# A hybrid decoder step on one core: selection steps moved from ahead of the first down projection to behind it, and one buffer for each part of the first group's up tiles

## The chip, the core and the metric

The kernel runs on one core of a Trainium2 chip. The core has TensorE (PE in the rows; PEld is its loading of weights), VectorE (DVE), ScalarE (ACT), GpSimd (POOL) and the queue of SyncE (SP), which here issues most of the transfers. The metric is the device time of one execution in microseconds (us). A profiled execution leaves a trace; its times count from the start of the span, which is the time from the first to the last instruction.

## The reference, cut to what matters

One layer of a decoder for a prompt of 1040 rows (16 of them learned) and 64 sample rows (8 sequences of 8): a recurrent branch and a sparse attention branch are merged through gates, projected and added to x; a gated feed-forward network with a causal convolution of width 3 follows. For each sample row the attention reads only the 256 past keys with the highest score.

```
def trunk_layer(x, pos, attend, shift_prev, s_prev, conv_prev, lp):
    h = rms_norm(x, lp['norm1_g']) @ lp['w_in']
    p_r, p_a, g_r, g_a = split_cols(h)
    y_r, s_fin, shift_last = rwkv7_branch(p_r, shift_prev, s_prev, lp)
    q, k, v, qi, wi, ki = dsa_project(p_a, pos)
    y_a = attend(q, k, v, qi, wi, ki)
    merged = (jax.nn.sigmoid(g_r) * (y_r @ lp['w_br_rwkv'])
              + jax.nn.sigmoid(g_a) * (y_a @ lp['w_br_attn']))
    x = x + merged @ lp['w_out']
    f, conv_last = conv_ffn(rms_norm(x, lp['norm2_g']), conv_prev, lp)
    x = x + f
...
def conv_ffn(h, conv_prev, lp):
    u = h @ lp['w_up']
    a, b = u[..., :D_FF], u[..., D_FF:]
    ext = jnp.concatenate([conv_prev.astype(a.dtype), a], axis=1)
    c = lp['conv_b'] + ext[:, 0:T] * lp['conv_w'][0]
    for j in range(1, CONV_W):
        c = c + ext[:, j:j + T] * lp['conv_w'][j]
    y = (jax.nn.gelu(c, approximate=False) * b) @ lp['w_down']
    return y, ext[:, T:]
...
    _, idx = lax.top_k(score, n_top)
```

D_MODEL is 1024, D_FF is 2816, everything is float32.

## The kernel before

The change lies in `tail`, the last part of the program, which runs from about 1395 us to the end. It works through the 1104 rows in three groups g of 368 columns (x is held transposed, so rows of x are columns here). For each group there are four stages on TensorE: the **branch** (16 products, two for each of the 8 channel tiles, merged by VectorE under the gates), the **projection** (8 output tiles, `out`; VectorE adds each to x in `project`), the **up tiles** (22 of them, f; each has a half a for the convolution and a half b) and the **down tiles** (8, t; VectorE adds each to x in `add_down`). After the projection and after the down tiles a norm is taken: ScalarE squares each tile, TensorE sums the squares over the partitions (`sum_tile`, L2177), ScalarE takes the root, VectorE inverts it and scales (`scale`). For the second norm of a group the sum of squares of down tile t stands in TensorE's order right behind down tile t + 1. In the second group the squares of tiles 1 to 5 are added on VectorE instead (`total`, L2927).

Every engine works off its own list of instructions in the order in which the code is written, and meets the others only through semaphores: nothing is reordered at run time. TensorE writes into three banks in turn, and a bank is free again when its reader has said so.

The **up tiles of the first group** are built otherwise than those of the second: all but the first are made of seven products of half size (`up_block`, L2295 and on), from sums of weights (WF) and of x (XF) that were made before. ScalarE takes the parts out of the banks into f1, f6, f5, f7, f4, f3 (`keep_block`), GpSimd adds them up into f16 and f167 and from these into the right half of a (AF) and the two halves of b (BC) (`finish_up`), ScalarE makes the three taps of the convolution from AF (`taps`), GpSimd adds the taps and multiplies by the gate. Each of the eight parts has two buffers, used in turn by even and odd f; AF has two as well, and its first two columns, which are the end of the group before (zero in the first group), are set to zero once.

The **selection** runs on VectorE beside all this. The scores of a sample row lie in two halves on 128 partitions, 4100 to a partition, and the 256 highest of each are found 8 at a time: 32 rounds of three steps, a maximum (L2878, MAX8), an index search (L2881, FIND_INDEX8 with its MATCH_VALUE_LOAD) and a replacement of the found values (L2884, MATCH_REPLACE8, with two small copies). That makes 96 steps, numbered 0 to 95; `steps(a, b)` writes the steps a to b - 1 into VectorE's list at that place. Behind step 95 stand the lists (`lists`), which turn indices into addresses; GpSimd carries parts of them over in the second group's up tiles, behind its work on tile f = 5 (LISTED) and the next, and TensorE transposes the result before up tile 14 (FLIP). GpSimd then gathers the keys and values, which TensorE uses from up tile 16 on.

The places of the steps before: 0 to 3 in the first group's branch, 4 to 10 in its projection, 11 to 61 behind its first norm (beside the up tiles of TensorE), 62 to 65 behind down tile 0, 66 to 77 two at a time behind the down tiles 1 to 6, 78 to 81 in the second group's branch, 82 to 84 in its projection behind tiles 1, 3 and 5, 85 to 95 behind its first norm.

## Time and profile before

| | |
|---|---|
| median of 3 runs | 2758.75 us (2757.34 to 2759.09) |
| the profiled execution | 2757.01 us |
| its span | 2755.2 us, 49283 instructions |
| TensorE busy | 2587.2 us, 94% |
| VectorE busy | 1738.1 us, 63% |
| ScalarE busy | 786.1 us, 29% |
| GpSimd busy | 390.5 us, 14% |
| maximum L2878, 32 times | 141.8 us, 4432 ns each |
| index search L2881, 32 times | 141.5 us, 4423 ns each |
| replacement L2884, 32 times | 141.2 us, 4413 ns each |

The busy times are sums over the whole span. Which engine sets the end differs from stage to stage, so they are to be read together with the chain of waits and with the timelines of a stage: in a timeline each row is an instruction, or several alike one after the other, with its start, its duration, and in brackets the idle time ahead of it on its engine and what ended that.

### The profile page before, as it was taken

The page shows a single profiled execution, that of the slowest core. Times are in us where ns is not written, and L with a number is a line of the kernel's source. Part 1 is how long each engine was busy: PE and PEld are TensorE (multiplying, and loading weights), DVE is VectorE, ACT ScalarE, POOL GpSimd, SP SyncE. Part 2 cuts the span into 40 slices and gives each one's busy share as a digit, 9 for nine tenths or more (in the row PEclk, how much of TensorE's full clock was granted, in tenths as well). Part 3 has the DMA queues.
Part 4 walks back from the last instruction along what each step waited for, and adds up shares of the span by engine and source line. Part 5 has one row for each costly group of instructions (what it writes and reads, how often), then busy time and mean ns, then how long its engine had stood idle before and what let it go on. Part 6 is the DMA issues. An engine that isn't in the chain of part 4 may idle for free.

```text
span 2755.2 us, 49283 instructions
## 1 busy us (share of the span) xinstructions
PE 2587.2 (94%) x19336; PEld 1784.8 (65%) x19336; DVE 1738.1 (63%) x3313; ACT 786.1 (29%) x1704; POOL 390.5 (14%) x575
## 2 busy tenths in 40 slices
PE   8998999999997997898899996899999999999997
PEld 5553566666654323788757995455665665679997
DVE  3555888864533457666679999967762322357666
ACT  2224322125443663111112551012334421122212
POOL 0000111000000000000002662000336451011111
PEclk9999999999998986999999998899999999999999
DMA  8882112131113540000245663244337563533332
GB/s 294 309 291 83 41 70 81 69 98 37 49 49 125 176 143 17 19 11 12 95 134 181 245 241 108 73 148 152 110 108 241 193 198 107 187 130 123 123 122 73
DMA packets 95959, 348.78 MB, mean 127 GB/s; under 512 B 19560, under 2 KB 43976, under 8 KB 74032
## 3 DMA queue, kind: packets, MB, share of 16 engines
q1 hardware_dynamic: 83696, 294.50, 31.1%
q0 software_dynamic: 12032, 51.14, 5.7%
q8 instruction: 153, 2.51, 0.4%
q14 instruction: 78, 0.64, 0.1%
HBM read 289.57 MB, written 55.23 MB: 125 GB/s over the span
## 4 chain that ended last, share of the span: by engine, by line
PE 43%; DVE 10%; DVEq 4%; issue 1%; DMA 1%; ACT 0%; POOL 0%; ACTq 0%; POOLq 0%; SPq 0%
PE banks L2359 6%; PE banks L2274 5%; PE banks L2292 5%; PE tl_P L2359 4%; DVE arena L2884 3%; DVE tl_v L2878 3%; DVEq L2882 3%; PE rc_P L1395 3%; PE tl_P L2274 2%; PE banks L2206 2%; PE banks L2218 2%; PE tl_P L2292 2%; PE banks L1407 1%; PE tl_P L2206 1%; PE tl_P L2417 1%
## 5 line engine op out<-in xcount | busy, mean ns | idle before, releaser
L437 PE MATMUL dp_PS<-base,dp_W 128*128 128x368 f32 x1440 | 465.9, 476 | 0.0
L437 PEld LDWEIGHTS dp_PS<-base,dp_W 128*128 128x128 f32 x1440 | 265.8, 190 | 157.5 <-issue 8.8
L162 PE MATMUL pa_PG<-pa_W,base 128*128 128x402 f32 (+1 forms) x576 | 199.1, 506 | 7.9 <-DMA pa_W<-in_w_dsa 7.9
L736 DVE TENSOR_SCALAR_CACHE_REDUCE dp_EQ<-dp_SCORE,dp_trial 128x1024 f32<-128x1024 f32 (+1 forms) x186 | 175.9, 946 | 19.9 <-issue 0.9
L162 PEld LDWEIGHTS pa_PG<-pa_W,base 128*128 128x128 f32 (+1 forms) x576 | 107.2, 187 | 94.7 <-issue 14.3
L2274 PE MATMUL banks<-base,tl_WU 128*128 128x368 f32 x496 | 158.8, 477 | 0.8 <-DVE base L2937 0.8
L2292 PE MATMUL banks<-base,tl_WD 128*128 128x368 f32 x484 | 156.2, 479 | 0.0
L2878 DVE MAX8 tl_v<-arena 128x8 f32<-128x4100 f32 x32 | 141.8, 4432 | 3.3 <-issue 1.5
L2881 DVE FIND_INDEX8 tl_i<-tl_v,arena 128x8 uint32<-128x4100 f32 x32 | 141.5, 4423 | 0.0
L2884 DVE MATCH_REPLACE8 arena<-tl_v,arena 128x4100 f32<-128x4100 f32 x32 | 141.2, 4413 | 0.3 <-issue 0.3
L2828 POOL DMA_INDIRECT arena<-in_cache_kv,tl_PHT x128 | 122.3, 955 | 109.7 <-PE tl_P L2438 73.6
L2274 PEld LDWEIGHTS banks<-base,tl_WU 128*128 128x128 f32 x496 | 94.4, 192 | 60.0 <-issue 3.6
L2292 PEld LDWEIGHTS banks<-base,tl_WD 128*128 128x128 f32 x484 | 91.6, 192 | 58.3 <-issue 5.9
L2543 ACT ACTIVATE arena<-base 128x368 f32<-128x368 f32 x44 | 22.1, 509 | 295.7 <-DVEq L2921 143.2
L814 DVE CUSTOM_DVE_ANT_0 dp_P<-dp_PS,dp_SCORE 128x1024 f32<-128x1024 f32 (+7 forms) x64 | 48.5, 758 | 66.7 <-PE dp_PS L487 58.8
L2304 PE MATMUL banks<-arena 128*128 128x184 f32 x504 | 85.6, 319 | 1.4 <-DVE arena L3052 1.4
L2218 PE MATMUL banks<-base,arena 128*128 128x368 f32 x256 | 81.2, 473 | 1.1 <-issue 1.1
L2304 PEld LDWEIGHTS banks<-arena 128*128 128x128 f32 x504 | 80.0, 190 | 1.6 <-issue 1.6
L2206 PE MATMUL banks<-arena 128*128 128x368 f32 x240 | 77.3, 473 | 2.0 <-DMA arena<-in_wb 1.2
L2274 PE MATMUL tl_P<-base,tl_WU 128*128 128x368 f32 x240 | 76.8, 473 | 0.0
L2510 POOL TENSOR_TENSOR base<-tl_T 128x368 f32<-128x368 f32 x36 | 30.3, 842 | 326.7 <-ACTq L2593 325.7
L594 ACT ACTIVATE dp_PMT<-dp_PS,dp_rest 128x368 f32<-128x368 f32 x42 | 23.8, 568 | 164.8 <-PE dp_PS L437 164.8
(525 smaller groups left out, 5057.4 us busy)
## 6 DMA issues: line engine op xcount, KB each, us to landing
tl_WU<-in_wu SPq DMA_DIRECT2D x58, 1024.0 KB, 4.9
pa_WQ<-in_wu SPq DMA_DIRECT2D x22, 1024.0 KB, 8.3
wsum<-pa_WS SPq DMA_DIRECT2D x22, 1024.0 KB, 4.9
tl_WD<-in_wd SPq DMA_DIRECT2D x32, 704.0 KB, 4.3
arena<-wsum SPq DMA_DIRECT2D x21, 1024.0 KB, 7.0
dp_W<-in_w_rw SPq DMA_DIRECT2D x15, 1024.0 KB, 4.9
arena<-in_wb SPq DMA_DIRECT2D x24, 512.0 KB, 3.7
arena<-in_wo SPq DMA_DIRECT2D x24, 512.0 KB, 3.8
```

The costliest lines, as they stand in the source:

```text
L162: last = pe.matmul(PG[0:n, c, 0:NC4], xT[:, k, r:r + n], W[:, c, k, :], start=k == 0, stop=k == KD - 1)
L437: last = pe.matmul(bank(f)[:, 0:w], W[:, t // 2 % 2, k, 128 * (t % 2):128 * (t % 2) + 128], xT[:, k, c:c + w], start=k == 0, stop=k == KD - 1)
L736: dve.tensor_scalar(EQ[0:n, 0:m], scored_of(j), values(n, x), None, op, ALU.add, accum_out=result[0:n, x:x + 1])
L2206: last = pe.matmul(out[:, 0:W], WM[:, i % 2, o:o + 128], YT[:, j, k, :], start=k == 0, stop=k == 3)
L2218: last = pe.matmul(out[:, 0:W], WM[:, i % 2, 128 * k:128 * k + 128], MT[:, k, :], start=k == 0, stop=k == KD - 1)
L2274: last = pe.matmul(out[:, 0:W], WU[:, i % 2, o:o + 128], XN[:, k, :], start=k == 0, stop=k == KD - 1)
L2292: last = pe.matmul(out[:, 0:W], WD[:, i % 3, 128 * e:128 * e + 128], HT[:, f, :], start=f == 0, stop=f == NF - 1)
L2304: last = pe.matmul(out[:, 0:H], weights[:, k, :], moving(k), start=first and k == 0, stop=k == 3, skip_group_check=True)
L2359: last = pe.matmul(out[:, 0:H], weights[:, k, :], moving(k), start=first and k == 0, stop=k == kk - 1, skip_group_check=True)
L2878: dve.max(v8[:, :], SC)
L2881: dve.max_index(i8[:, :], v8[:, :], SC)
L2884: dve.match_replace(SC, v8[:, :], SC, TAKEN)
```

## The change

Three things change; the work itself stays the same.

- **Steps.** 11 to 51 stand behind the first group's first norm (41 steps instead of 51), 52 to 72 three at a time behind the down tiles 0 to 6 (21 instead of 16), 73 to 76 in the second group's branch (4 as before), 77 to 83 one at a time behind tiles 0 to 6 of its projection (7 instead of 3), 84 to 95 behind its first norm (12 instead of 11).
- **Buffers.** f1, f6, f5, f7, f4, f3, f16 and f167 have one buffer each. ScalarE waits before it writes f1 of a tile until GpSimd has made f167 of the tile before (the new semaphore `f_mid`), and before it writes f5 until GpSimd has finished BC of the tile before (`b_read`). Before, one wait at the head of `keep_block` asked for the tile before the last.
- **First columns of AF.** They are copied from AL on ScalarE for every tile, in `taps`; the setting to zero on GpSimd is gone. AL is zero in the first group.

The functions now take the group as an argument, and a table `UPS = (NF, 1)` says in which group the seven products are used. With these values that is the first group alone, as before, and every bank and every transfer stays as it was.

```
+UPS = (NF, 1)
...
-        "PF": arena[:, 11872:14816].rearrange("p (i a n) -> p i a n", i=8, a=2),
-        "AF": arena[:, 14816:15556].rearrange("p (a n) -> p a n", a=2),
+        "PF": arena[:, 14048:15520].rearrange("p (i n) -> p i n", i=8),
+        "AF": arena[:, 15520:16260].rearrange("p (a n) -> p a n", a=2),
...
-                def taps(f):
-                    s = f % 2
+                def taps(g, f):
+                    s, i = f % 2, NF * g + f
                     w0, w1, w2, cb = (cw[:, k, f:f + 1] for k in range(4))
-                    if f >= 2:
-                        act.wait_ge(convolved, f - 1)
-                    act.wait_ge(f_right, f)
+                    act.activation(AF[:, s, 0:2], AL[:, f, :], ACT.Copy)
+                    if i >= 2:
+                        act.wait_ge(convolved, i - 1)
+                    act.wait_ge(f_right, block_no(g, f))
                     act.drain()
...
-                def keep_block(f):
-                    s = f % 2
-                    if f >= 3:
-                        act.wait_ge(b_read, f - 1)
-                    keep(f1[:, s, :], FA, fa_made, fa_taken, 2 * f - 1)
+                def keep_block(g, f):
+                    s, m = f % 2, block_no(g, f)
+                    FA, FD, FB = banks_of(g)
+                    if m > 1:
+                        act.wait_ge(f_mid, m - 1)
+                    keep(f1, FA, fa_made, fa_taken, 2 * m - 1)
                     if f > 1:
-                        taps(f - 1)
-                    keep(f6[:, s, :], FB, fb_made, fb_taken, 2 * f - 1)
-                    keep(f5[:, s, :], FD, fd_made, fd_taken, 2 * f - 1)
...
+                        taps(g, f - 1)
+                    keep(f6, FB, fb_made, fb_taken, 2 * m - 1)
+                    act.wait_ge(b_read, NF * g + f)
+                    keep(f5, FD, fd_made, fd_taken, 2 * m - 1)
...
-                pool.memset(AF[:, :, 0:2], 0.0)
...
-                    pool.tensor_tensor(f167[:, s, :], f1[:, s, :], f7[:, s, :], ALU.add)
-                    pool.drain()
...
+                        pool.tensor_tensor(f167, f1, f7, ALU.add)
+                        pool.drain().then_inc(f_mid, 1)
...
                             if g == 1:
-                                steps(78 + u // 4, 79 + u // 4)
+                                steps(73 + u // 4, 74 + u // 4)
...
-                            if g == 1 and t % 2 == 1:
-                                steps(82 + t // 2, 83 + t // 2)
+                            if g == 1:
+                                steps(77 + t, 78 + t)
...
-                        steps(11, 62)
+                        steps(11, 52)
...
-                        steps(85, 96)
+                        if UPS[1] > 1:
+                            mix_rows(XF, xf_done, False)
+                        steps(84, 96)
...
-                            if t == 0:
-                                steps(62, 64)
                             if t < KD - 1:
-                                steps(64 + 2 * t, 66 + 2 * t)
+                                steps(52 + 3 * t, 55 + 3 * t)
```

The order of VectorE's instructions shows where the steps stand. Line numbers after the change are 23 higher here (L2878 is L2901, L2881 is L2904, L2884 is L2907, `add_down` L2920 is L2943, `project` L2914 is L2937, `total` L2927 is L2950). Around the additions of the first group's down tiles 0, 1 and 2 VectorE has, before:

```order
L2881 MAX_INDEX tl_i<-tl_v,arena 128x8
L2920 TENSOR_TENSOR base<-base,tl_P 128x368
L2884 MATCH_REPLACE arena<-tl_v,arena 128x4100
L2885 COPY arena<-tl_v 128x8
L2886 CAST arena<-tl_i 128x8
L2878 MAX tl_v<-arena 128x8
L2881 MAX_INDEX tl_i<-tl_v,arena 128x8
L2884 MATCH_REPLACE arena<-tl_v,arena 128x4100
L2885 COPY arena<-tl_v 128x8
L2886 CAST arena<-tl_i 128x8
L2920 TENSOR_TENSOR base<-base,banks 128x368
L2878 MAX tl_v<-arena 128x8
```

Tile 0 is added behind step 61 and four steps follow. VectorE has there, after:

```order
L2901 MAX tl_v<-arena 128x8
L2943 TENSOR_TENSOR base<-base,tl_P 128x368
L2904 MAX_INDEX tl_i<-tl_v,arena 128x8
L2907 MATCH_REPLACE arena<-tl_v,arena 128x4100
L2908 COPY arena<-tl_v 128x8
L2909 CAST arena<-tl_i 128x8
L2901 MAX tl_v<-arena 128x8
L2943 TENSOR_TENSOR base<-base,banks 128x368
```

Tile 0 is added behind step 51, ten steps sooner, and between two additions stands one whole round. In the second group's projection VectorE has from tile 1 to tile 4, before:

```order
L2914 TENSOR_TENSOR base<-arena,banks 128x368
L2881 MAX_INDEX tl_i<-tl_v,arena 128x8
L2914 TENSOR_TENSOR base<-arena,banks 128x368
L2927 TENSOR_TENSOR tl_TOTAL<-tl_TOTAL,arena 128x368
L2914 TENSOR_TENSOR base<-arena,tl_P 128x368
L2927 TENSOR_TENSOR tl_TOTAL<-tl_TOTAL,arena 128x368
L2884 MATCH_REPLACE arena<-tl_v,arena 128x4100
L2885 COPY arena<-tl_v 128x8
L2886 CAST arena<-tl_i 128x8
L2914 TENSOR_TENSOR base<-arena,banks 128x368
```

A step stands behind every second tile. VectorE has from tile 1 to tile 4, after:

```order
L2937 TENSOR_TENSOR base<-arena,banks 128x368
L2901 MAX tl_v<-arena 128x8
L2937 TENSOR_TENSOR base<-arena,banks 128x368
L2950 TENSOR_TENSOR tl_TOTAL<-tl_TOTAL,arena 128x368
L2904 MAX_INDEX tl_i<-tl_v,arena 128x8
L2937 TENSOR_TENSOR base<-arena,tl_P 128x368
L2950 TENSOR_TENSOR tl_TOTAL<-tl_TOTAL,arena 128x368
L2907 MATCH_REPLACE arena<-tl_v,arena 128x4100
L2908 COPY arena<-tl_v 128x8
L2909 CAST arena<-tl_i 128x8
L2937 TENSOR_TENSOR base<-arena,banks 128x368
```

A step stands behind every tile.

## Rows read from the trace of the kernel before

**Rows 1.** Chain of waits in order of time: start us, us, what.

```profile
1694.44 4.43 DVE tl_v L2878
...
1708.24 4.43 DVE tl_v L2878
...
1752.49 13.61 PE tl_P L2292 x44
```

**Rows 2.** Timeline of TensorE, first group's down tiles 1 to 4.

```profile
1687.57 13.77 PE L2292 MATMUL banks<-base,tl_WD 128*128 128x368 f32 x44
1732.34 1.59 PE L2177 MATMUL tl_P<-arena,tl_ones 128*128 128x368 f32 x2 [31.00 <-ACT arena L2543]
1733.72 15.61 PE L2292 MATMUL banks<-base,tl_WD 128*128 128x368 f32 x44
...
1752.33 13.77 PE L2292 MATMUL tl_P<-base,tl_WD 128*128 128x368 f32 x44
...
1766.55 13.77 PE L2292 MATMUL banks<-base,tl_WD 128*128 128x368 f32 x44
```

**Rows 3.** Timeline of VectorE, the same stage to its last addition.

```profile
1685.23 4.42 DVE L2881 FIND_INDEX8 tl_i<-tl_v,arena 128x8 uint32<-128x4100 f32 x1
...
1731.11 0.54 DVE L2920 TENSOR_TENSOR base<-base,tl_P 128x368 f32<-128x368 f32 x1
1731.86 0.09 DVE L2884 MATCH_VALUE_LOAD arena<-tl_v,arena 128x8 f32 x1 [0.21 <-issue]
...
1823.02 0.54 DVE L2920 TENSOR_TENSOR base<-base,banks 128x368 f32<-128x368 f32 x1 [4.25 <-PE banks L2292]
```

**Rows 4.** Timeline of VectorE, the second group's projection.

```profile
1871.84 0.54 DVE L2914 TENSOR_TENSOR base<-arena,tl_P 128x368 f32<-128x368 f32 x1
...
1887.08 0.09 DVE L2884 MATCH_VALUE_LOAD arena<-tl_v,arena 128x8 f32 x1
...
1891.87 0.54 DVE L2914 TENSOR_TENSOR base<-arena,banks 128x368 f32<-128x368 f32 x1
...
1895.56 0.54 DVE L2914 TENSOR_TENSOR base<-arena,banks 128x368 f32<-128x368 f32 x1 [2.40 <-PE banks L2218]
...
1896.97 4.43 DVE L2878 MAX8 tl_v<-arena 128x8 f32<-128x4100 f32 x1
1901.55 0.54 DVE L2914 TENSOR_TENSOR base<-arena,tl_P 128x368 f32<-128x368 f32 x1
...
1905.46 0.54 DVE L2914 TENSOR_TENSOR base<-arena,banks 128x368 f32<-128x368 f32 x1 [2.61 <-PE banks L2218]
```

**Rows 5.** Timeline of TensorE, the second group's up tile 16.

```profile
2074.51 1.15 PE L2417 MATMUL tl_P<-ident,arena 128*128 128x128 f32 x8 [2.53 <-DMA arena<-in_cache_kv,tl_PHT]
2075.45 6.76 PE L2274 MATMUL banks<-base,tl_WU 128*128 128x368 f32 x16
```

**Rows 6.** Busy time by stretch: PE, PEld, DVE, ACT, POOL, PEclk, DMA share, GB/s.

```profile
2076.00:2077.00 1.00, 1.00 (x3) 0.65 (x2) 0.00 (x0) 0.75 (x3) 0.69 (x2) 0.50 0.97 385
```

**Rows 7.** Timelines of VectorE and GpSimd, the first list's hand-over.

```profile
1967.38 0.29 DVE L2946 TENSOR_SCALAR arena<-arena 64x256 f32<-64x256 f32 x1
...
1971.81 0.96 POOL L2526 TENSOR_TENSOR base<-base 128x368 f32<-128x368 f32 x1 [0.24 <-issue]
1973.40 0.64 POOL L2815 DMA_DIRECT2D arena<-arena  x1 [0.62 <-issue]
```

**Rows 8.** Timelines of GpSimd and ScalarE, an up tile of the first group.

```profile
1559.09 0.58 POOL L2804 TENSOR_TENSOR arena<-arena 128x184 f32<-128x184 f32 x1 [0.18 <-issue]
...
1560.98 0.58 POOL L2791 TENSOR_TENSOR base<-arena 128x184 f32<-128x184 f32 x1
...
1560.82 0.33 ACT L2609 ACTIVATE arena<-tl_P 128x184 f32<-128x184 f32 x1 [0.98 <-PE tl_P L2304]
...
1562.82 0.19 ACT L2621 ACTIVATE tl_AL<-arena 128x2 f32<-128x2 f32 x1
1563.11 0.54 ACT L2609 ACTIVATE arena<-banks 128x184 f32<-128x184 f32 x2
```

More of the change, by code:

```diff
@@ L1954, in tail @@
         f1, f6, f5, f7, f4, f3, f16, f167 = (M["PF"][:, i] for i in range(8))
-        FA, FD, FB, FE = R2, R0, R1, K0
-        FREED_D, FREED_B, FREED_A = 0, 1, 2
+        by_seven = lambda g, f: 1 <= f < UPS[g]
+        plain = [(g, f) for g in range(2) for f in range(NF) if not by_seven(g, f)]
+        nth = lambda g, f: plain.index((g, f)) + 1
+        block_no = lambda g, f: f if g == 0 else UPS[0] - 1 + f
+        FE = K0
         LROW = WU[:, :, :].rearrange("p i n -> p (i n)")[:, 0:3 * D].rearrange("p (b n) -> p b n", b=3)
@@ L1993, in tail @@
             if g < 2:
-                order += [(x, g, f) for f in range(NF if g else 1) for x in "ab"] + [("down", g, t) for t in range(KD)]
+                order += [(x, g, f) for f in range(NF) if not by_seven(g, f) for x in "ab"] + [("down", g, t) for t in range(KD)]
         use = {k: n for n, k in enumerate(order)}
@@ L2003, in tail @@
         uses = [sum(1 for n in use.values() if n % 3 == r) for r in range(3)]
-        uses0 = [sum(1 for n in use.values() if n % 3 == r and n <= use["b", 0, 0]) for r in range(3)]
+        uses0 = lambda g, r: sum(1 for n in use.values() if n % 3 == r and n <= use["b", g, 0])
+        nth_bank = lambda g, n: (use["a", g, 0] + n) % 3
+        banks_of = lambda g: [RB[nth_bank(g, n)] for n in (2, 0, 1)]
         NBL = len(BLOCKS3)
@@ L2138, in _ @@
                         load_up(NF * g + 1)
-                    if g == 0:
-                        load_sums(1)
-                        load_sums(2)
+                    if g < 2 and UPS[g] > 2:
+                        load_sums(g, 1)
+                        load_sums(g, 2)
                     if g:
@@ L2718, in _ @@
                         continue
-                    if g == 0:
-                        read_a(0, 0)
-                        read_b(0, 0)
-                        for f in range(1, NF):
-                            keep_block(f)
-                        taps(NF - 1)
-                    for f in range(NF if g else 0):
+                    if UPS[g] > 1:
+                        read_a(g, 0)
+                        read_b(g, 0)
+                        for f in range(1, UPS[g]):
+                            keep_block(g, f)
+                        taps(g, UPS[g] - 1)
+                    for f in range(UPS[g] if UPS[g] > 1 else 0, NF):
                         if g == 1 and f >= F0:
@@ L2806, in _, with finish_up @@
-                finish_up(NF - 1)
-                conv_add(pool, 0, NF - 1)
-                gate_up(pool, 0, NF - 1)
-                for f in range(BY_POOL):
-                    conv_add(pool, 1, f)
-                    if f:
-                        gate_up(pool, 1, f - 1)
+                def finish_up(g, f):
+                    s, m = f % 2, block_no(g, f)
+                    pool.wait_ge(fd_taken, 2 * m)
+                    pool.tensor_tensor(AF[:, s, 2 + H:2 + W], f16, f3, ALU.add).then_inc(f_right, 1)
+                    pool.tensor_tensor(BC[:, s, half[1]], f167, f5, ALU.add)
+                    pool.wait_ge(fe_taken, m)
+                    pool.tensor_tensor(BC[:, s, half[0]], f167, f4, ALU.add)
+                    pool.drain().then_inc(b_read, 1)
@@ new lines, in up_tiles @@
+                def up_tiles(g):
+                    for f in range(1, UPS[g]):
+                        m = block_no(g, f)
+                        if f > 1:
+                            finish_up(g, f - 1)
+                        pool.wait_ge(fa_taken, 2 * m - 1)
+                        pool.wait_ge(fb_taken, 2 * m - 1)
+                        pool.tensor_tensor(f16, f1, f6, ALU.add)
+                        conv_add(pool, g, f - 1)
+                        gate_up(pool, g, f - 1)
+                        pool.wait_ge(fb_taken, 2 * m)
+                        pool.tensor_tensor(f167, f1, f7, ALU.add)
+                        pool.drain().then_inc(f_mid, 1)
+                        if g == 1:
+                            hand_on(f)
+                    finish_up(g, UPS[g] - 1)
+                    conv_add(pool, g, UPS[g] - 1)
+                    gate_up(pool, g, UPS[g] - 1)
@@ L2813, in _, with hand_on @@
+                def hand_on(f):
                     if f == LISTED:
@@ L2820, in _ @@
                         pool.dma_start(K2[64:128, :], key[:, 128:256]).then_inc(spread, 16)
-                gate_up(pool, 1, BY_POOL - 1)
+                up_tiles(0)
+                if UPS[1] > 1:
+                    up_tiles(1)
+                for f in range(BY_POOL if UPS[1] <= 1 else 0):
+                    conv_add(pool, 1, f)
+                    if f:
+                        gate_up(pool, 1, f - 1)
+                    hand_on(f)
+                if UPS[1] <= 1:
+                    gate_up(pool, 1, BY_POOL - 1)
                 pool.wait_ge(placed_list, 1)
```

127 lines of the change are left out of this document (58 added, 69 removed).

## The prediction

> **What bounds the kernel now.** I read the chain of waits first, in order of time [rows 1]. Up to the first group's down projection, and after it, the chain lies mostly on TensorE (PE in the rows). Through the first group's up tiles and beyond it lies on VectorE (DVE), on one maximum, index search and replacement of the selection after the other, of which rows 1 show two maxima; it comes back to TensorE's down tiles only at 1752.49. The second view is TensorE's own timeline of those tiles [rows 2]. Down tile 1 starts at 1687.57, so tile 0's product was complete then. Tile 1 ends near 1701.2, and the next instruction, tile 0's sum of squares (L2177), starts at 1732.34 after 31.00 us of idle time. The third view says why [rows 3]: the addition of tile 0 (L2920) runs at 1731.11 on VectorE, 43.5 us after its product was there, because `steps(11, 62)` stands ahead of it in VectorE's order. From there to the sum of squares of the last tile, VectorE's additions set the pace and then catch up: the addition of tile 7 starts at 1823.02, with TensorE again the slower one. So the stage to cost runs from 1685 to 1823, and the question is what the moved steps do in the places that they go to.
>
> **The down tiles of the first group: 33.0 us gained.** In the changed order the loop ahead of tile 0 ends after step 51, a maximum. The next step, an index search, began at 1685.23 [rows 3], so VectorE is free then, 2.3 us before tile 0 is complete; TensorE's up tiles ahead of it are not moved. The addition of tile 0 comes at about 1687.8 and the 31.00 us are gone. Behind each of the tiles 0 to 6 there are now three steps, one whole round. A round takes 1708.24 - 1694.44 = 13.80 us [rows 1], the addition with its hand-over 1731.86 - 1731.11 = 0.75 us [rows 3]; with 0.05 for the end of the last step I take 14.6 us a tile. TensorE needs 1766.55 - 1752.33 = 14.22 us a tile [rows 2], and 0.6 less for the first, which has no sum of squares. So VectorE now sets the pace, by 0.4 us a tile. The addition of tile 7 starts at 1687.8 + 7 x 14.6 = 1790.0 instead of 1823.02: 33.0 us. Were TensorE alone in it, that would be 1687.8 + 13.6 + 6 x 14.22 = 1786.7; the round of steps costs 3.3 us of what could be had. A round with a tenth more in it, from a stall in fetching instructions, makes 32.3; I keep 32.3 to 33.4.
>
> **The second group's branch: nothing.** Four steps before and four now, 78 to 81 against 73 to 76. The kinds differ by one maximum that becomes an index search, 4.43 us [rows 4] against 4.42 [rows 3].
>
> **The second group's projection: 7.7 us lost.** Here three steps become seven, one behind each of the tiles 0 to 6. On before's clock tile 0's addition (L2914) starts at 1871.84 [rows 4]. Prices from the same rows: a replacement up to the next addition 1891.87 - 1887.08 = 4.79, a maximum 1901.55 - 1896.97 = 4.58, an index search taken like the maximum at 4.6; an addition alone 0.75, and with the running total 1896.97 - 1895.56 = 1.41. The order from tile 0 on is replacement, maximum, index search, replacement, maximum, index search, replacement, with totals from tile 2 on: 5.54 + 5.33 + 6.01 + 6.20 + 5.99 + 6.01 + 6.20 = 41.3 us. The addition of tile 7 then starts at 1871.9 + 41.3 = 1913.2, against 1905.46 before. TensorE has its eight products ready at the old pace, so the whole 7.7 us lie on the path: the sum of squares, the root, the scaling and the first up tile of the second group all wait for that addition. Only the loads of x and of the output weights stand behind VectorE too, and they lead by a tile or more.
>
> **TensorE's clock: 4.2 us lost, the least certain term.** Both lags make TensorE wait with nothing to do, about 4 us before the second group's branch and about 8 us (in two pieces) before its up tiles. Such waits are seen in the trace: after 2.53 us of idle time before 2074.51 the next 16 matmuls took 6.76 us, where 44 take 13.77 (so 16 take 5.0), and the granted clock was 0.50, the 1.2 GHz level [rows 5, 6]. After the 31.00 us, 44 matmuls took 15.61 instead of 13.77 [rows 2]. So one such wait costs 1.7 to 1.8 us if nothing covers it. I take 1.2 for the first, as the branch's first products have a little room while VectorE scales, and 3.0 for the second, since the transposes of the row output and then the first up tile run at the lower level one after the other. Bounds: 0, if the clock stays; 8, if each wait costs twice 1.8 and VectorE's work behind it slips too. The sum goes by 4.2.
>
> **One step more behind the scaling: nothing.** Twelve steps instead of eleven stand ahead of the lists, so the first instruction of the lists moves from 1967.38 to about 1972.0 on the stage's own clock [rows 7]. What takes the list up is GpSimd (POOL), which works off a convolution and a gate until 1971.81 + 0.96 = 1972.8 and issues its transfer at 1973.40 [rows 7]. The cover is some 0.4 us; beyond it the lists would slip by what is over, and TensorE meets them only nine up tiles later.
>
> **One buffer each for the parts of the up tiles: nothing.** ScalarE (ACT) now waits twice a tile for GpSimd. The second sum of parts ends at 1559.09 + 0.58 = 1559.67, and ScalarE writes f1 again at 1560.82; the last half of BC is done at 1560.98 + 0.58 = 1561.56, and f5 is written after 1563.11 [rows 8]. So the new waits are met 1.1 and 1.5 us early. The added copy of two columns is like L2621, 0.19 us [rows 8]; it shifts ScalarE and then GpSimd by about that and leaves 0.9 and 1.3 us. What would be late next is TensorE's second product into the same bank. The price with no cover is 21 tiles times what is missing. The Trainium skill speaks against this edit: its front page, "Trainium Kernel Development and Optimization", section Best Practices, says to double-buffer for performance, overlapping transfers with compute. By that rule every tile would show a wait; by the rows the reader has finished before the writer comes, and the sum goes by the rows.
>
> **Sum.** 33.0 - 7.7 - 4.2 = 21.1 us. The profiled execution took 2757.01 us, of which the span is 2755.2 and the rest lies around it, unchanged; that makes 2735.9. The median of the runs, 2758.75, is 1.7 above it, which makes 2737.7, say 2738 us.
>
> **Rivals.** (A) *The clock stays up* or the slow matmuls are all hidden: 25.3 us gained, 2733.5. For it: TensorE has some room behind both waits. Against: 2.53 us of idle time was enough [rows 5]. (B) *VectorE is later than costed*: rounds of 14.0 instead of 13.8 and a projection in which the slower clock and the steps add up, 8 us in place of 4.2 for the clock and 2 us more of lag: about 15 us gained, 2744. (C) *Another wait stands behind the removed one*: the weights of the down tiles, three buffers deep, might not arrive at 14.2 us a tile, and TensorE would wait for them instead. The tiles from 1752.33 on run at that pace without such a wait [rows 2], so this is unlikely; it would leave within 0.2% of the old time. (D) *Slower, by the single buffers*: if ScalarE met GpSimd's new signals late on every tile, TensorE's up tiles would stretch. One microsecond on each of 21 tiles eats the 21.1; at 2 us a tile the time is 2758.75 + 42 - 21 = 2780. Against it stand margins of 0.9 and 1.3 us. (E) *It does not do what it says*: TensorE still idles at tile 1. The order of instructions shows the ten steps gone from ahead of tile 0, so I give it no share of its own beside C.
>
> **How the numbers follow.** Forecast, 2735 to 2742: 0.55. A: 0.22. B: 0.14. C: 0.04. D: 0.05, of which one part in five ends within 0.2%. A difference of 0.2%, 5.5 us, is about what a measurement of this kernel can tell from none. So faster 0.91, within 0.2% 0.05, slower 0.04. The range takes in the forecast, most of A and most of B: 2731 to 2746.
>
> **What would show it.** In the profile after: no idle time of tens of microseconds at the second or third down tile; three selection steps between two additions of down tiles, the additions some 14.6 us apart; the last of them about 3 us behind TensorE; one step between two additions of the projection, 5.3 to 6.2 us apart, and an idle stretch of TensorE of some 8 us before the row transposes; granted clock 0.50 there and at the start of the second group's up tiles; the list's transfer issued at the same distance from the up tiles as before; the up tiles of the first group still without idle time of TensorE. The prediction is wrong if ScalarE waits for GpSimd in the up tiles, if the down tiles wait for their weights, or if the projection's lag does not reach the up tiles.

## The result, and the profile after

| | before | after |
|---|---|---|
| median of the runs | 2758.92 us (4 runs) | 2736.24 us (4 runs) |
| ratio of the means of the runs | | 0.9912, 95% interval 0.9894 to 0.993 |
| the profiled execution, its span | 2757.01, 2755.2 us | 2736.69, 2734.9 us |

Faster by 22.7 us, by the medians; forecast were 21.1 us and 2738 us. One execution of the kernel with the larger fill ("What the clock costs") took 5314.92 us and is left out of the time given there. The head of the page after and its chain of waits, shares of the span by engine:

```profile
span 2734.9 us, 49325 instructions
PE 2589.1 (95%) x19336; PEld 1788.2 (65%) x19336; DVE 1739.7 (64%) x3313; ACT 788.5 (29%) x1725; POOL 391.4 (14%) x574
...
PE 47%; DVE 7%; DVEq 3%; issue 1%; DMA 1%; POOL 0%; ACT 0%; POOLq 0%; ACTq 0%; SPq 0%
```

The busy times are those of before to within 3 us; what has gone is waiting. Lines have moved: L2901, L2904 and L2907 are the maximum, the index search and the replacement, L2943 the addition of a down tile, L2937 that of a projection tile, L2184 a sum of squares, L2299 the down products.

TensorE in the first group's down tiles (start, duration, operation, in brackets the idle time ahead of it), which answers to [rows 2]:

```profile
1702.99 0.78 PE L2184 MATMUL tl_P<-arena,tl_ones 128*128 128x368 f32 x2
1703.61 13.77 PE L2299 MATMUL banks<-base,tl_WD 128*128 128x368 f32 x44
1717.21 0.78 PE L2184 MATMUL tl_P<-arena,tl_ones 128*128 128x368 f32 x2
...
1793.07 1.16 PE L2184 MATMUL tl_P<-arena,tl_ones 128*128 128x368 f32 x2 [3.96 <-ACT arena L2553]
1794.02 4.10 PE L2213 MATMUL banks<-arena 128*128 128x368 f32 x8
1797.96 2.64 PE L2213 MATMUL tl_P<-arena 128*128 128x368 f32 x8
```

The 31.00 us ahead of the first sum of squares are gone; tile follows tile every 14.22 us. In their place stands one wait of 3.96 us ahead of the last sum. Behind it the branch's first 8 products take 4.10 us, the next 8 take 2.64: the lower and the full clock, as the windows further down show.

VectorE in the same stage, which answers to [rows 3], and in the projection, which answers to [rows 4]:

```profile
1682.15 4.43 DVE L2901 MAX8 tl_v<-arena 128x8 f32<-128x4100 f32 x1
1689.59 0.54 DVE L2943 TENSOR_TENSOR base<-base,tl_P 128x368 f32<-128x368 f32 x1 [3.01 <-PE tl_P L2299]
...
1704.15 0.54 DVE L2943 TENSOR_TENSOR base<-base,banks 128x368 f32<-128x368 f32 x1
...
1791.84 0.54 DVE L2943 TENSOR_TENSOR base<-base,banks 128x368 f32<-128x368 f32 x1
...
1841.35 0.54 DVE L2937 TENSOR_TENSOR base<-arena,tl_P 128x368 f32<-128x368 f32 x1
...
1882.75 0.54 DVE L2937 TENSOR_TENSOR base<-arena,banks 128x368 f32<-128x368 f32 x1
```

Step 51 ends at 1686.58, VectorE is idle for 3.01 us, and then the additions run 14.56 us apart, the time of one round of steps and one addition (once 14.90, where VectorE pauses for 0.43 us ahead of a maximum). In the projection the eight additions take 1882.75 - 1841.35 = 41.40 us, where before they took 33.62 [rows 4].

TensorE from the end of the projection to the second group's first up tile (L2281), and its clock in the branch's first products and there (columns as in [rows 6]; the granted clock is the third number from the end):

```profile
1877.92 0.89 PE L2196 MATMUL tl_P<-tl_TOTAL,tl_ones 128*128 128x368 f32 x2 [3.12 <-DVEq L2951]
...
1883.97 1.59 PE L2184 MATMUL tl_P<-arena,tl_ones 128*128 128x368 f32 x2 [4.15 <-ACT arena L2553]
1885.36 1.06 PE L2239 MATMUL banks<-ident,base 128*128 128x128 f32 x4
...
1891.39 5.18 PE L2281 MATMUL banks<-base,tl_WU 128*128 128x368 f32 x16 [0.78 <-DVE base L2960]
```

```profile
1794.00:1796.00 2.00, 2.00 (x5) 1.16 (x4) 1.07 (x1) 1.97 (x3) 0.00 (x0) 0.50 0.00 0
1797.00:1799.00 2.00, 2.00 (x8) 1.25 (x7) 1.92 (x4) 1.34 (x3) 0.00 (x0) 1.00 0.00 0
...
1880.00:1885.00 5.00, 1.03 (x2) 0.73 (x3) 3.14 (x4) 1.57 (x2) 0.00 (x0) 0.50 0.00 0
1888.00:1889.00 1.00, 1.00 (x7) 1.00 (x6) 0.66 (x1) 0.00 (x0) 0.00 (x0) 0.50 0.85 315
1890.00:1892.00 2.00, 1.22 (x6) 0.84 (x7) 1.36 (x3) 0.64 (x2) 0.00 (x0) 1.00 0.57 212
```

The two idle pieces are 3.12 and 4.15 us. The clock is at the lower level through the last sum and most of the transposes (L2239), but full again before the up tile, whose 16 products take 5.18 us.

**Where the time went.** The same marks in all traces (the start of the first group's first down product, of VectorE's additions, and of the second group's first up product and first attention product) cut the changed stages into pieces, in us. They do not depend on what lay ahead: the profiled executions reach the first product of this part of the program anywhere from 1392.3 to 1400.0 us, though none of the kernels differs ahead of it but for idle time that one of them fills. That is 7.7 us, where the times after spread over 5.4 (2732.71 to 2738.07). So terms of a few us are read from the pieces.

| | first down product to addition 7 | to the projection's addition 0 | to its addition 7 | to the first up product | sum | from there to attention |
|---|---|---|---|---|---|---|
| before | 149.13 | 48.82 | 33.62 | 7.88 | 239.45 | 161.17 |
| after | 116.13 | 49.51 | 41.40 | 8.64 | 215.68 | 161.87 |
| difference | -33.00 | +0.69 | +7.78 | +0.76 | -23.77 | +0.70 |

### The profile page after: what moved, and what is told of

Its sections match the earlier page's. It is cut to its first block, busy times and chain, and to the rows that moved or that the text cites. A ratio compares the mean times of both kernels' runs of the same rounds, so it can differ in the third digit from the quotient of the medians.

```text
span 2734.9 us, 49325 instructions
## 1 busy us (share of the span) xinstructions
PE 2589.1 (95%) x19336; PEld 1788.2 (65%) x19336; DVE 1739.7 (64%) x3313; ACT 788.5 (29%) x1725; POOL 391.4 (14%) x574
## 4 chain that ended last, share of the span: by engine, by line
PE 47%; DVE 7%; DVEq 3%; issue 1%; DMA 1%; POOL 0%; ACT 0%; POOLq 0%; ACTq 0%; SPq 0%
PE banks L2368 6%; PE banks L2281 5%; PE tl_P L2368 4%; PE banks L2313 4%; PE banks L2299 3%; PE tl_P L2313 3%; PE rc_P L1395 3%; PE banks L2213 3%; PE tl_P L2281 2%; DVE arena L2907 2%; DVEq L2905 2%; PE tl_P L2299 2%; DVE tl_v L2901 1%; PE tl_P L2213 1%; PE banks L1407 1%
## 5 line engine op out<-in xcount | busy, mean ns | idle before, releaser
L2281 PE MATMUL banks<-base,tl_WU 128*128 128x368 f32 x496 | 157.9, 475 | 0.8 <-DVE base L2960 0.8
L2299 PE MATMUL banks<-base,tl_WD 128*128 128x368 f32 x484 | 154.3, 474 | 0.0
L2901 DVE MAX8 tl_v<-arena 128x8 f32<-128x4100 f32 x32 | 141.8, 4431 | 3.4 <-issue 1.6
L2904 DVE FIND_INDEX8 tl_i<-tl_v,arena 128x8 uint32<-128x4100 f32 x32 | 141.5, 4423 | 0.0
L2907 DVE MATCH_REPLACE8 arena<-tl_v,arena 128x4100 f32<-128x4100 f32 x32 | 141.3, 4414 | 0.0
L2281 PEld LDWEIGHTS banks<-base,tl_WU 128*128 128x128 f32 x496 | 94.0, 191 | 59.5 <-issue 2.8
L2299 PEld LDWEIGHTS banks<-base,tl_WD 128*128 128x128 f32 x484 | 90.5, 190 | 57.1 <-issue 3.7
L2281 PE MATMUL tl_P<-base,tl_WU 128*128 128x368 f32 x240 | 76.8, 473 | 0.0
```

Source lines behind the costliest of these rows:

```text
L2281: last = pe.matmul(out[:, 0:W], WU[:, i % 2, o:o + 128], XN[:, k, :], start=k == 0, stop=k == KD - 1)
L2299: last = pe.matmul(out[:, 0:W], WD[:, i % 3, 128 * e:128 * e + 128], HT[:, f, :], start=f == 0, stop=f == NF - 1)
L2901: dve.max(v8[:, :], SC)
L2904: dve.max_index(i8[:, :], v8[:, :], SC)
L2907: dve.match_replace(SC, v8[:, :], SC, TAKEN)
```

## Experiments

**The steps or the buffers.** Two kernels, one with each half of the change.

Steps alone:

```
-steps(11, 62)
+steps(11, 52)
...
-steps(64 + 2 * t, 66 + 2 * t)
+steps(52 + 3 * t, 55 + 3 * t)
...
-if g == 1 and t % 2 == 1: steps(82 + t // 2, 83 + t // 2)
+if g == 1: steps(77 + t, 78 + t)
```

> The kernel before with nothing changed but the places of the selection steps; every part of the up tiles keeps its two buffers. Theory (the whole change of time is that of the steps): as the changed kernel, about 22.5 us under the kernel before, 2736 us, within 3 us. Rival (the single buffers cost or give something): the time differs from the changed kernel's by more than 3 us, faster if ScalarE waits for GpSimd in the up tiles after the change, slower if the buffers were part of the gain; the first group's up stage then differs from the 185.7 us that it took after the change.

Buffers alone, the diff of the change without those lines:

> The changed kernel with the selection steps back at their old places: only the single buffers and the copied columns are left. Theory: the time of the kernel before, 2759 us, within 2 us, and an up stage of the first group within 0.5 us of the old 185.3. Rival (the new waits are met late): one microsecond a tile makes 21 us, 2780 us, and TensorE shows idle time on every up tile.

Measured: the steps alone 2733.59 us, ratio 0.9905 (0.989 to 0.9919), and 215.65 us from the first down to the first up product; the buffers alone 2758.9 us, ratio 1.0 (0.9991 to 1.001), and 239.07 us. The up stages lasted 198.37 us with the steps alone and 197.44 with the buffers alone, against 198.22 after and 197.72 before (from the first up product on; the expectations count from a later mark), so what differs there does not go with the buffers. The whole gain is that of the steps. The changed kernel run once more, beside later experiments:

> The changed kernel once more, beside the two runs below on the same chip. Theory: 2736 us, 0.991 of the kernel before; 215.7 us from the first down tile of the first group to the second group's first up tile, 118.3 of them down tiles and 56.3 projection, as the stretches did not differ by more than 0.5 us between runs that share their steps.

It took 2735.39 us, 0.9919 (0.9905 to 0.9933), with 215.51 us in the stretch.

**How near the single buffers are to costing something.** Three more additions on GpSimd in each of the first group's up tiles but the first; nobody reads them.

```
 pool.tensor_tensor(f167, f1, f7, ALU.add)
+for i in range(3):
+    pool.tensor_tensor(M["rest"][:, H * i:H * i + H], f1, f7, ALU.add)
 pool.drain().then_inc(f_mid, 1)
```

> The changed kernel with three more additions on GpSimd, each 0.58 us, in every up tile of the first group, between the second sum of parts and the signal that ScalarE waits for before it writes f1 again; nobody reads their result. Theory (the single buffers cost nothing as long as GpSimd is 0.9 us early for f1 and 1.3 us early for f5, and what is over comes once a tile): 1.7 us later leaves 0.8 us uncovered in each of 20 tiles, an up stage some 16 us longer, 2752 us, with TensorE idle in each tile. Rival (there is more room behind those margins, on ScalarE or in the banks): less than 5 us, 2741 us at most. Rival (GpSimd is then the bound itself): 20 us and more.

One run took 2752.42 us, 2752 were expected. The up stage grew from 198.22 to 216.53 us, by 18.3. Waits of ScalarE and TensorE there (waiter, what it waited for: us in total, times, longest), with the three additions:

```profile
ACT arena L2619 <- POOLq L2820: 44.8, 20, 2.8
...
PE banks L2313 <- ACT arena L2619: 13.9, 20, 1.1
```

and in the same stage of the changed kernel:

```profile
ACT arena L2619 <- POOLq L2818: 1.2, 1, 1.2
...
PE banks L2313 <- DVE arena L3075: 1.4, 1, 1.4
```

L2820 (L2818 in the changed kernel) is the signal f_mid. With the additions ScalarE waits for it 44.8 us in all and TensorE for ScalarE 13.9 us, in 20 tiles, which is most of the 18.3; without them ScalarE meets it late once, by 1.2 us, and TensorE does not wait for ScalarE. So rival D was a real mechanism: with GpSimd 1.7 us later a tile is 0.9 us longer. The other 0.8 us were covered, near the margin of 0.9 that the prediction left; where exactly the cost starts, one point does not show.

**VectorE's lag in two places.** Two steps more ahead of the first down tile, into the 3.01 us of idle time and the slack behind it:

```
-steps(11, 52)
+steps(11, 54)
...
-steps(52 + 3 * t, 55 + 3 * t)
+steps(54 + 3 * t, min(57 + 3 * t, 73))
```

> The changed kernel with two more steps (52 and 53) ahead of the first group's down tiles, so that 53 to 72 is what stands behind the tiles 0 to 6 from 54 on, the last tile with one step instead of three. Theory (after the change VectorE's total work between the product of tile 0 and the addition of tile 7 sets the pace, and it had 3.01 us with nothing to do ahead of the first addition): the addition of tile 0 comes about 5.8 us late, which TensorE does not need before its sum of squares at the end of tile 1; the addition of tile 7 comes as early as TensorE allows, 3 us sooner than after the change, and the 1 us of the slower clock behind it goes too: about 4 us less, 2732 us. Rival (a step ahead of tile 0 costs what it takes, as the ten steps did before): TensorE idles at its sum of squares of tile 0, and the time is the changed kernel's or up to 9 us more, 2736 to 2745 us.

Two steps fewer in the projection:

```
-BY_POOL, LISTED, FLIP, F0 = 14, 5, 14, 16
+BY_POOL, LISTED, FLIP, F0 = 14, 6, 14, 16
...
-if g == 1:
+if g == 1 and t < 5:
     steps(77 + t, 78 + t)
...
-steps(84, 96)
+steps(82, 96)
```

> The changed kernel with two of the seven steps taken out of the second group's projection (those behind tiles 5 and 6) and put behind its norm, where 14 stand then instead of 12; the hand-over of the list on GpSimd moves one up tile later with them. Theory (the two steps behind the last tiles are the lag of VectorE that TensorE waits for): the idle time of 3.12 and 4.15 us ahead of the row transposes goes, the addition of tile 7 comes about 7.8 us sooner, and with the slower clock behind it that makes 8.5 us, 2728 us. Rival (the list is then late): the gather or the transpose of the list holds TensorE up in the second group's up tiles, and up to 9 us of the gain are given back there, 2736 us, with a new idle time at the transpose before up tile 14 or at the attention after up tile 16.

Both together:

> Two more steps ahead of the first group's down tiles and two fewer in the second group's projection, both edits together. Each alone took 3.6 us (115.11 instead of 118.31 from the first down tile to the branch, and 0.4 in the branch) and 6.5 us off the stretch from the first down tile to the second group's first up tile, which lasted 215.68 us after the change. Theory (two separate lags of VectorE, which add up): 205.5 us for that stretch, 10 us under the changed kernel, 2726 us. Rival (one lag hides the other, since VectorE has the same 96 steps to do): 209 us or more, 2729 us or more.

| | time, us | ratio to before | to the down tiles' addition 7 | to the projection's addition 0 | to its addition 7 | to the first up product | sum | from there to attention |
|---|---|---|---|---|---|---|---|---|
| two ahead | 2731.48 | 0.9902 (0.9887 to 0.9918) | 113.16 | 48.89 | 41.38 | 8.64 | 212.07 | 161.82 |
| five in the projection | 2730.34 | 0.9896 (0.988 to 0.9912) | 116.13 | 49.26 | 33.55 | 10.20 | 209.14 | 162.72 |
| both | 2724.0 | 0.9869 (0.9852 to 0.9887) | 113.16 | 48.88 | 33.55 | 10.16 | 205.75 | 163.37 |

The times of the first two cannot be told from the changed kernel's; the pieces can. Two steps ahead of tile 0, VectorE and then TensorE's sum of squares:

```profile
1694.48 0.54 DVE L2943 TENSOR_TENSOR base<-base,tl_P 128x368 f32<-128x368 f32 x1
...
1701.54 0.78 PE L2184 MATMUL tl_P<-arena,tl_ones 128*128 128x368 f32 x2
```

The addition of tile 0 comes 6.3 us later within the stage (20.22 instead of 13.88 us behind the first down product), TensorE's sum shows no idle time, and addition 7 comes 3.0 us sooner. That is most of the 3.3 us that the prediction gave as what the steps cost over TensorE alone. With both edits the pieces add up as the first theory had it, 205.75 us against 205.5, and the time is 12 us under the changed kernel's, of which the pieces explain 8.4 (9.93 less in the stretch, 1.50 more up to attention). The intervals of the two ratios do not overlap: this is a better place for the steps than either kernel has.

One piece went the other way. With five steps in the projection the waits ahead of the sums are gone, but addition 7 to the first up product takes 10.20 us. TensorE there, and ScalarE, which copies the transposed rows out:

```profile
1886.69 1.10 PE L2239 MATMUL banks<-ident,base 128*112 128x128 f32 x4 [3.20 <-ACTq L2571]
1888.58 6.81 PE L2281 MATMUL banks<-base,tl_WU 128*128 128x368 f32 x16 [0.79 <-DVE base L2960]
...
1885.94 0.60 ACT L2569 ACTIVATE tl_YROW<-banks 128x512 f32<-128x512 f32 x1 [3.25 <-DMA out_y<-tl_YROW]
```

ScalarE waits 3.25 us for the first row output to leave its buffer, TensorE for ScalarE, and the first up tile runs at the lower clock.

**Why that row output is late.** First theory: it meets the weights of the up tiles on the DMA engines. This and the next two kernels have both edits of the steps.

```
 load_x(KD * g + t)
+if g == 1 and t in (4, 5):
+    load_up(NF + t - 4)
...
-if g < 2:
+if g == 0:
     load_up(NF * g)
     load_up(NF * g + 1)
```

> Both edits of the steps together, and the first two transfers of the second group's up weights are issued behind the x transfers of projection tiles 4 and 5 instead of behind that of tile 7. With five steps in the projection alone, the row outputs were issued 7.04 us after those weights (15.65 us in the changed kernel), ScalarE waited 3.25 us for the first of them, TensorE 3.20 us, and the first up tile's 16 products took 6.81 instead of 5.18 us. Theory (the output transfer shared the DMA engines with the weights): with the weights landed early the wait is 1.3 us again, the first up tile is back at 5.2 us, and from the last addition of the projection to the first up tile it takes 8 us instead of 10.2: about 3 us less than both edits alone. Rival (the output transfer was slow by itself): the wait stays. Rival (the early weights hold up the x and output weights): additions of projection tiles 5 to 7 come later by 1 us or more, and the time is that of both edits or above.

The same two loads much earlier:

```
 for i in range(2 * KD):
     load_down(2 * KD * g + i)
+if g == 0:
+    load_up(NF)
+    load_up(NF + 1)
...
-if g < 2:
+if g == 0:
     load_up(NF * g)
     load_up(NF * g + 1)
```

> Both edits of the steps together, and the first two transfers of the second group's up weights are issued behind the last down weights of the first group, ahead of the branch's own loads, at a time when the queue has nothing to do for some 28 us afterwards. Theory (the row outputs shared the DMA engines with these weights, and the earlier try moved the collision to the output weights, where TensorE waited 0.42 us and the additions came 0.8 us later): from the first to the last addition of the projection 33.6 us as with the two edits alone, and from there to the first up tile 8.1 us or less instead of 10.2; 203.5 us from the first down tile to the first up tile instead of 205.75, 2722 us. Rival (nothing is gained for the whole): what TensorE wins there it waits for at the gather of keys and values, which hangs on VectorE's lists: the stretch from the first up tile to the first attention product gets as much longer, 165.6 instead of 163.4 us, and the time stays at 2724 us.

Behind the x transfers: 2725.06 us, 0.987 (0.9852 to 0.9887); TensorE's wait ahead of the last transposes fell from 3.16 to 1.33 us as the theory had it, but the projection's additions took 34.37 us, with TensorE waiting 0.42 us for its output weights, and 204.20 us in all. Ahead of the branch: 2722.28 us, 0.9864 (0.9849 to 0.9879), and 206.22 us, with 10.60 from addition 7 to the up product: the output is late although no weights are near it. The theory falls, though the time is the 2722 us that it forecast. None of these times can be told from that of both edits alone (0.9852 to 0.9887). What the late outputs have in common is in the DMA traffic around them (bandwidth in 40 slices of the 7 us from 1871, then queues and issues: KB each, median us to landing), here with the weights ahead of the branch:

```profile
GB/s 0 0 0 0 0 0 0 0 0 0 0 0 117 351 363 351 223 281 456 351 363 47 0 12 0 12 12 23 23 23 23 35 23 0 0 0 0 0 0 0
...
q8 instruction: 1, 0.02, 0.8%
...
out_y<-tl_YROW SPq DMA_DIRECT2D x3, 256.0 KB, 4.1
```

and around the same outputs with the weights behind the x transfers (7 us from 1875; no transfer of instructions in it):

```profile
q1 hardware_dynamic: 500, 0.93, 35.9%
...
out_y<-tl_YROW SPq DMA_DIRECT2D x4, 256.0 KB, 2.0
```

After 2 us at 220 to 460 GB/s the first has a tail of 2 us at 12 to 35 GB/s; the first two outputs land after 4.3 and 4.1 us instead of 2.0. A transfer of instructions (queue q8) lies among them at 1874.2, 1.9 us behind the first issue. With five steps alone and with both edits it lay 1.0 to 1.1 us behind it, with the same tail. In before, after, with two steps ahead and with the weights behind the x transfers it came 5.3 to 5.7 us behind the first issue, and the first four outputs landed in 2.0 us. So I moved TensorE's stream of instructions:

```
+for i in range(16):
+    pe.transpose(PY[:, 0:128], ident[:, :], ident[:, :])
 for g in range(3):
     branch(g)
```

> Both edits of the steps together, as they were, and 16 transposes that nobody reads ahead of the first product of the whole stretch (before 1397 us), where TensorE waited 1.45 us anyway. They take about 2 us and move everything behind them by 16 places in TensorE's stream of instructions. In the three runs in which the first two row outputs landed late (3.8 to 4.3 us after the issue instead of 2.0) a transfer of instructions fell within 1.5 us of their issue, and the bandwidth then had a tail of 2 to 3 us at 12 to 35 GB/s; in the runs before, after, with two steps ahead alone and with the early weights that transfer came 5 us or more later, and the outputs landed in 2.0 us. Theory (that transfer of instructions delays the outputs): it falls ahead of the outputs now, ScalarE waits 1.3 us, and from the last addition of the projection to the first up tile it takes 8.1 us instead of 10.16; from the first down tile to the first up tile 203.7 us instead of 205.75. Rival (the outputs are late for another reason, which the five steps in the projection bring along): the instruction transfer is elsewhere and the wait of 3.2 us stays, 205.8 us.

TensorE had 1.45 us of idle time where these stand. The transfer of instructions came at 1874.4, 0.2 us ahead of the first issue (1874.62), the first two outputs landed after 2.3 and 2.1 us, ScalarE waited 1.62 us, addition 7 to the up product took 8.34 us and the whole stretch 203.58, close to the theory's 8.1 and 203.7. The time did not follow: 2725.71 us, 0.9878 (0.9861 to 0.9894), no different from both edits alone. The first up tile ran at the lower clock all the same (7.88 us), and TensorE waited 3.25 us at the gather of keys and values, 164.59 us to attention. That a transfer of instructions among the outputs delays them is borne out by all fourteen traces: the first two outputs took 3.7 to 4.3 us in the three in which it lies 1.0 to 1.9 us behind the first issue, and 2.0 to 2.3 us in the eleven in which it lies elsewhere. But the one edit made to test it moved it by 1.2 us only, and how it delays them no run shows. Whose instructions it carries the traces tell: between two transfers on that queue TensorE runs 256 to 258 weight loads and matmuls on the mean, in each of the fourteen traces, while VectorE runs anything from 13 to 143 instructions in that of the changed kernel. So they go with TensorE's stream.

**What the clock costs.** Products that nobody reads, in the waits of the changed kernel:

```
+def spin(count):
+    for i in range(count):
+        pe.matmul(PY[:, 0:W], ones[:, :], HT[:, 0, :], start=True, stop=True)
...
+if n == 1 and t == KD - 1:
+    spin(12)
...
+if n == 2:
+    spin(9)
...
+if n == 2 and t == KD - 1:
+    spin(12)
```

They stand ahead of the last sum of squares of the down tiles, of the projection's total and of its last sum.

> The changed kernel with products that nobody reads put into TensorE's three waits for VectorE's lag: 12 ahead of the last sum of squares of the down tiles, 9 ahead of the total and 12 ahead of the last sum of the projection, into a bank that is idle there. They take about 0.31 us each and fill 3.7, 2.8 and 3.7 of the 3.96, 3.12 and 4.15 us of idle time, so that TensorE hardly pauses. Theory (the lower clock cost 1.45 us in all, read off the stretches): the granted clock is 1.0 in the branch's first products and in the row transposes, 0.7 us less from the last addition of the down tiles to the first of the projection, 0.8 us less up to the first up tile, in all 1.5 us, 2735 us. Rival (the prediction's 4.2 us for the clock): 4 us less, 2732 us. Rival (the products end late): 49.51 and 8.64 us of those stretches get longer instead.

Each product was two passes of 0.31 us, so they filled twice the waits and ended late: 2739.77 us, 0.9928 (0.9913 to 0.9943), and the pieces were 51.75 and 12.33 us instead of 49.51 and 8.64. With 6, 4 and 6:

> The changed kernel with products that nobody reads in TensorE's three waits, 6, 4 and 6 of them instead of 12, 9 and 12: each turned out to be two passes of 0.31 us, so that the first try filled 7.4, 5.6 and 7.4 us and ended late. These fill 3.7, 2.5 and 3.7 of the 3.96, 3.12 and 4.15 us. Theory (the lower clock cost 1.45 us in these stretches): the granted clock stays at 1.0 into the branch and through the row transposes; from the last addition of the down tiles to the first of the projection 48.8 us instead of 49.5, from the last addition of the projection to the first up tile 7.9 instead of 8.6. Rival (the prediction's 1.2 and 3.0 us): 48.3 and 5.6 us, or as much less spread over the first up tile. What stays open: with the larger fill the first up tile ran at the lower level all the same (6.57 us for 15 products), though TensorE had not paused before the transposes; if it does so again, the fall at that place is not the doing of the waits filled here.

TensorE with the smaller fill (L2189 are the added products, L2223 the branch, L2291 the up tile):

```profile
1789.46 3.87 PE L2189 MATMUL tl_P<-base,tl_ones 128*128 128x368 f32 x12
1793.58 0.89 PE L2184 MATMUL tl_P<-arena,tl_ones 128*128 128x368 f32 x2 [0.25 <-ACT arena L2563]
1794.30 2.64 PE L2223 MATMUL banks<-arena 128*128 128x368 f32 x8
...
1884.58 0.60 PE L2249 MATMUL banks<-ident,base 128*128 128x128 f32 x4
...
1890.51 5.18 PE L2291 MATMUL banks<-base,tl_WU 128*128 128x368 f32 x16 [0.79 <-DVE base L2970]
```

The branch starts with 2.64 us for 8 products, the transposes take 0.60 instead of 1.06, and the pieces are 48.89 and 7.87 us: 0.62 and 0.77 less, 1.39 us in all, and 214.28 us for the stretch. The time, 2736.45 us and 0.9917 (0.9904 to 0.9931), can't show so little.

## Why the prediction was right, and which term was off

- **Down tiles, 33.0 us gained:** measured 33.00, and its parts came out too: addition 0 13.88 us behind the first product (13.91 by the sum), the seven rounds 102.25 us (7 x 14.6 = 102.2). The 0.4 us a tile by which VectorE sets the pace, 3.3 us in all, were there: two steps moved into the idle time ahead of tile 0 gave 3.0 of them back. That idle time, 3.01 us, had been in the sum as 2.3 and was not put to use in it.
- **Branch, nothing:** with the wait filled so that the clock stays up, or without the lag, the piece to the projection's addition 0 is 48.9 us, against 48.82 before.
- **Projection, 7.7 us lost:** measured 7.78, each of the seven intervals within 0.07 us of its price, and all of it on the path: with five steps the additions took 33.55 us.
- **Clock, 4.2 us lost:** this term was mis-sized. The traces give 0.69 + 0.76 = 1.45 us, the filled waits 1.39. Of the 1.2 us for the branch 0.69 were there, of the 3.0 at the second place 0.76. The room in the branch that the prediction gave as its reason was there: the slow sum and products put TensorE 1.7 us behind, and the kernel before waits 0.81 us for VectorE a little later in the branch (at 1833.36), a wait that is gone after. The second had taken a slow first up tile into the sum; that tile was not slow (5.18 us, as before), since the clock was full again by the end of the transposes. The sum was taken from an up tile with only 1.15 us of transposes between the wait and the slow products [rows 5], which the prediction did not mention; here a sum and the transposes came between, 7.4 us in all. The 2.75 us less for the clock, and 0.08 more for the projection, are what lies between the forecast 21.1 and the 23.77 us of the stretch: 33.00 - 7.78 - 1.45 = 23.77. The profiled executions differ by 20.3, since the one after came 1.8 us later to the stretch and lost 0.7 us up to attention and 0.9 in the rest; kernels that are alike in those stages differ as much. So it is chance that the totals, 22.7 us by the medians and 20.3 by the profiled executions, came nearer to 21.1 than the stretch did. Rival A, with 25.3 us and no loss for the clock, was nearer to the stretch's gain, but only in part for its reason: the clock did fall, and the slow products were hidden in good part, not all.
- **One step more behind the scaling, nothing:** GpSimd's transfer of the list was issued 60.24 us behind the first up product instead of 60.06, and the gather at 148.12 us in both. The cover of 0.4 us was used up: GpSimd waited 0.79 us for the list.
- **Single buffers, nothing:** shown by the buffers alone, 1.0 (0.9991 to 1.001). The Trainium skill, "Trainium Kernel Development and Optimization", section Best Practices, says to double-buffer for performance, so that transfers overlap with compute. These buffers are filled by ScalarE and not by transfers, so the sentence did not bear on them, and that every tile would show a wait was the prediction's own reading. One buffer was enough here because GpSimd had read the old part before ScalarE brought the new one; with GpSimd 1.7 us later it cost 18.3 us.
- **The other rivals.** B, later steps: a round with its addition took 14.56 us in six of seven, 13.81 without the 0.75, where 13.85 was costed. C, weights of the down tiles arriving late: no wait for them among the tiles. E: the 31.00 us are gone.

## What to carry to other kernels

Work that is moved off the path comes back on it where it is put: count at each new place what the engine has to do from one hand-over to the next, and compare it with the engine that waits; an excess of 0.3 to 0.4 us a tile added up to 3 us at the last one, and four steps more among the projection's tiles cost 8. The slack at the first hand-over, idle time ahead of it plus the time until its result is needed, is worth filling first. What a lower clock costs has to be read where it falls: ahead of the branch and on short transposes it was under 1 us each, on a full up tile 1.6 to 2.7.

## What the runs showed of the hardware

**At the same pattern of work the clock fell in one kernel's trace and not in another's.** TensorE's rows from the sums to the first up tile are alike in the kernel before and in the one with early weights: the same sums and transposes, with idle times of 0.27, 1.33 and 0.79 us. The first kept the full clock, in the second it fell, from 1.00 to 0.50, ahead of the first up tile, which took 7.86 us instead of 5.18 (columns as in [rows 6]; before, then early weights):

```profile
1913.00:1915.00 2.00, 1.67 (x6) 1.10 (x7) 2.00 (x5) 0.86 (x2) 0.00 (x0) 1.00 0.56 201
```

```profile
1882.00:1884.00 2.00, 2.00 (x4) 1.16 (x5) 2.00 (x5) 1.53 (x4) 0.00 (x0) 0.50 0.41 127
```

With the larger fill the up tile was slow too, though TensorE had not paused before the transposes:

```profile
1893.90 6.88 PE L2291 MATMUL banks<-base,tl_WU 128*128 128x368 f32 x16 [0.79 <-DVE base L2970]
```

In all five kernels with five steps in the projection that tile took 6.81 to 7.88 us instead of 5.18, which gives back up to 2.7 us of what they gain. Its cause stays open.

**A 16 KB transfer of TensorE's instructions, begun 1.0 to 1.9 us behind the issue of the first of two 256 KB outputs,** went with landings after 3.7 to 4.3 us instead of 2.0 to 2.3, in three traces of fourteen. Such a transfer came once for every 256 to 258 weight loads and matmuls of TensorE on the mean.
